# Tile-0 exponentials, the pacing of the second tail and the routing schedule of a one-core decoder block moved

## The chip, the cores and the metric

One core of a Trainium2 chip runs the whole program. The metric is the device time of one execution in microseconds (us); the time before is the median of three runs.

## The reference

One hybrid decoder layer on 512 tokens of width 2048, all in float32. Cut to what matters here:

```python
h = rms_norm(x, g[0]) * (1 + scale1) + shift1
y = hybrid_mixer(h, ...)              # attention + convolution branches, sigmoid gates, w_out
x = x + gate1 * rms_norm(y, g[1])
h = rms_norm(x, g[2]) * (1 + scale2) + shift2
q = h @ w_q                           # 8 heads, two halves of 128
s1, s2 = q halves @ sub_keys          # 128 scores each
v1, i1 = top_k(s1, 16); v2, i2 = top_k(s2, 16)
top, ci = top_k(v1[:, None] + v2[None, :], 16)
expert = i1[ci // 16] * 128 + i2[ci % 16]
gate = softmax(top)
act = gelu(h . expert_down[expert]) * gate      # 128 experts for each token
y = sum(act * expert_up[expert])
x = x + gate2 * rms_norm(y, g[3])
```

For each of the 512 tokens 128 rows of `expert_down` and 128 rows of `expert_up`, of 8 KB each, are gathered from memory: 2 x 512 gathers of 1 MB.

## The kernel before

The program has a first part (projections, attention, convolution) that the change doesn't touch, and then, on each of five engines, an order written out by hand.

**Two tails.** `tail(0)` does the rest of the mixer, the norms, the queries and the key scores for the first 128 tokens (tile 0), `tail(1)` the same for the other 384 (tiles 1 to 3). A tail reads its weights in chunks of 1 MB (0.5 MB for `ao`): four times the groups `ga` (4 chunks), `gc` (4), `ao` (2), `co` (2), then `out` (16), `x` (one for each tile), and then the queries `q`: 16 chunks. In `tail(1)` the queries come twice: `q` for tile 1 (16 chunks in four groups, each followed by the scores `sc` of two heads) and `q2` for tiles 2 and 3 (16 more). That is 99 chunks. SyncE issues them into a ring of three buffers in `tail(1)`; a buffer comes free when TensorE has used it.

**Retrieval.** It runs over 512 blocks `b`, 128 for each tile. For each block GpSimd gathers a row set from `down` (into `d_row`) and, 22 blocks later in its own order, one from `up` (into `u_row`). VectorE does `dot(b)` on `d_row`, line 1633; ScalarE the gelu of 16 dots and the weights (`block_weights`, line 1170); TensorE `weighted_rows(b - 24)` on `u_row`. GpSimd's queue is in order: a gather that waits holds all behind it. A `down` gather waits for the dot that last used its buffer and, at the first 32 blocks of a tile, for the routing of the heads that it needs (`routed`); an `up` gather waits for TensorE's use of its buffer. Both rings have three buffers up to block `WIDE` and five after it, and block `WIDE` itself waits for the end of `tail(1)`. At every 32nd block TensorE and ScalarE (line 1158) lay out the next 32 tokens of `h`, after all dots of the 32 before.

**Routing.** `route(t, n, step)`, six steps, takes two heads of tile `t` from scores to expert numbers on VectorE; step 3 releases ScalarE's `gate_exp(t, n)` (line 1151), and `gates(t, n)` on VectorE (lines 1619 to 1624) waits for that exponential. Tiles 0 and 1 are routed inside their tails; tiles 2 and 3 in `retrieve`, between dots, from the 28th block of the tile before on, with 24 blocks for each pair of heads.

**Pacing.** All engines place the retrieval inside `tail(1)` by one table: behind chunk `i` of `tail(1)` each goes on to block `PACE[i]` (`passed`, `chunk_out`). ScalarE goes by lumps of 3, 4 and 5 chunks, VectorE by lumps of 9, 2 and 1 in the gate groups and 4 in the queries. Before, `PACE` is 6, 8, 16, 19, 21 behind chunks 2, 3, 8, 10 and 11, 118 behind the last `x` chunk, 120, 123, 125 and 128 behind the four `q` groups, and 156 behind the last `q2` group.

**End of tail(0).** VectorE ends it with `route(0, 3)`, `gates(0, 2)` and `gates(0, 3)`, and then goes on to `tail(1)`, whose first act is `passed(1, 9)`: the first dots. ScalarE's `gate_exp(0, 3)` stands behind the four `ga` sigmoids (line 1222) of the first group of `tail(1)`. TensorE's `co` group of each round of four waits for VectorE's products on the `ao` group (line 1700), which stand behind the dots of `passed(c, 9)`.

Of the kernel before, what the change touches and what calls it, by code (L numbers as in the profile page):

```python
# [20 lines left out]
TT = S // P  # L21
# [15 lines left out]
def tail_groups(c):  # L37

    out = [(kind, cg, k) for cg in range(4) for kind, k in (("ga", 4), ("gc", 4), ("ao", 2), ("co", 2))]
    out += [("out", i, 4) for i in range(4)] + [("x", t, 1) for t in range(TAIL[c][1] // P)]  # L40
    for go, _, _ in QUERIES[c]:
        out += [(kind + go, i, k) for i in range(4) for kind, k in (("q", 4), ("sc", 0))]
    return out
# [3 lines left out]
BLOCKS = GROUPS * 32  # L47
LAG = 24
UP_LAG = 22
WIDE = 160  # L50
END = BLOCKS + 64


C_ID = 0
# [77 lines left out]
def block_pace():  # L132


    work = [k * (12 if kind in ("ga", "gc", "co", "out") else 6 if kind == "ao" else 9 if kind == "x" else 4) / max(k, 1)
            for kind, _, k in tail_groups(1) for _ in range(k)][:-16]
    out = [round(128 * at / sum(work)) for at in itertools.accumulate(work)]
    return out + [128 + 7 * (i + 1) // 4 for i in range(16)]


PACE = block_pace()
# [60 lines left out]
def block_kernel(nc, x, ada_w, ada_rows, w_in, w_attn_o, w_conv_o, w_out, w_q, down, up, keysT, pos, small, const, out):  # L202
# [9 lines left out]
    with ctx:  # L212
# [808 lines left out]
        def _(act):  # L1021
# [126 lines left out]
            def gate_exp(t, n):  # L1148
                act.wait_ge(gap2_ready, 4 * t + n + 1)
                g_ = gate[:, 2 * n:2 * n + 2, :]  # L1150
                A(g_, g_, ACT.Exp).then_inc(exp2_ready, 1)
# [32 lines left out]
            def retrieve(upto):  # L1184
                nonlocal pos_
                while pos_ < upto:
                    b = pos_
                    if b % 32 == 0 and b < BLOCKS:
                        h2_quarters(b // 32)
                    unit = b // 16 - 1  # L1190
                    if 0 <= 16 * unit < BLOCKS:
                        if b % 16 == 3:
                            unit_gelu(unit)
                        if 7 <= b % 16 < 15:
                            block_weights(16 * unit + 2 * (b % 16 - 7))
                            block_weights(16 * unit + 2 * (b % 16 - 7) + 1)
                    J = b // 32 - 1
                    if 0 <= J < GROUPS and b % 32 == 24:
                        z_squares(J)
                    if 0 <= J < GROUPS and b % 32 == 26:  # L1200
                        z_std(J)
                    t, n = b // 128 + 1, (b % 128 - 44) // 24
                    if 2 <= t < TT and b % 128 >= 44 and (b % 128 - 44) % 24 == 0 and n < 4:
                        gate_exp(t, n)
                    pos_ += 1

            chunk_at = 0
# [7 lines left out]
            def tail(c):  # L1215
                t0, n = TAIL[c]
                tok = slice(t0, t0 + n)
                for cg in range(4):
                    passed(c, 3)
                    for m in range(4):  # L1220
                        act.wait_ge(g_done, DONE[c, "ga", cg] + m + 1)
                        A(mixT[:, mix_at(4 * cg + m), tok], ps[:, m, 0:n], ACT.Sigmoid).then_inc(act_took, 1)
                    if c == 0 and cg == 0:
                        conv_activation()
                    if c == 1 and cg == 0:
                        gate_exp(0, 3)
                    passed(c, 4)
                    for m in range(4):
                        act.wait_ge(g_done, DONE[c, "gc", cg] + m + 1)
                        if c or cg:  # L1230
                            act.wait_ge(mix_ready, 16 * c + 4 * cg)
                        elif m == 0:
                            act.wait_ge(lnsq_done, 1)
                        A(sgc[:, m, 0:n], ps[:, m, 0:n], ACT.Sigmoid).then_inc(act_took, 1)
                    if c == 0 and cg == 0:
                        for t in range(TT):
                            attention_turned(t)
                    passed(c, 5)
                for i in range(4):
                    passed(c, 3)  # L1240
                    for m in range(4):
                        act.wait_ge(g_done, DONE[c, "out", i] + m + 1)
                        A(hT[:, 4 * i + m, tok], ps[:, m, 0:n], ACT.Copy)
                        if i == 0 and m == 0:
                            act.wait_ge(mix_ready, 16 * (c + 1))
                        if i and m == 0:
                            act.wait_ge(sqs_used, 10 * c + i)
                        A(sqt[:, m, 0:n], ps[:, m, 0:n], ACT.Square).then_inc(act_took, 1)
                    passed(c, 1)
                act.wait_ge(ss_done, 2 * c + 1)  # L1250
                A(row[:, 0:n], ps[:, 6, 0:n], ACT.Sqrt, scale=1.0 / D, bias=eps).then_inc(std2_ready, 1)
                passed(c, n // P)
                act.wait_ge(dve_took, VTOOK[c, "x", n // P - 1] + 4)
                for kk in range(8):
                    if kk >= 2:
                        act.wait_ge(sqs_used, 10 * c + 3 + kk - 1)
                    A(sqt[:, 2 * (kk % 2):2 * (kk % 2) + 2, 0:n], mixT[:, 2 * kk:2 * kk + 2, tok], ACT.Square).then_inc(sq2_ready, 1)  # L1257
                act.wait_ge(ss_done, 2 * c + 2)
                A(row[:, 0:n], ps[:, 6, 0:n], ACT.Sqrt, scale=1.0 / D, bias=eps).then_inc(std2_ready, 1)
                for k in range(KT):  # L1260
                    act.wait_ge(h2n_ready, 4 * c + k // 4 + 1)
                    A(hT[:, k, tok], hT[:, k, tok], ACT.Identity, scale=modc[:, 2, k:k + 1], bias=modc[:, 1, k:k + 1]).then_inc(h2_ready, 1)  # L1262
                for go, q0, qn in QUERIES[c]:
                    for i in range(4):
                        passed(c, 3)
                        for m in range(4):
                            act.wait_ge(g_done, DONE[c, "q" + go, i] + m + 1)
                            if m == 0 and i:
                                act.wait_ge(g_done, DONE[c, "sc" + go, i - 1] + 4)
                            elif m == 0 and go:  # L1270
                                act.wait_ge(g_done, DONE[c, "sc", 3] + 4)
                            A(sqt[:, m, 0:qn], ps[:, m, 0:qn], ACT.Copy).then_inc(act_took, 1)
                        for m in range(4):
                            act.wait_ge(g_done, DONE[c, "sc" + go, i] + m + 1)
                            for t in range(q0 // P, (q0 + qn) // P):
                                ins = A(sc[t][:, 4 * i + m, :], ps[:, m, t * P - q0:(t + 1) * P - q0], ACT.Copy)
                            ins.then_inc(act_took, 1)
                        passed(c, 1)
                        if not go and i:
                            gate_exp(c, i - 1)  # L1280
                    if c and not go:
                        gate_exp(c, 3)
                if c == 0:
                    act.wait_ge(g3_done, 1)
                    A(g3r, ps[:, 7, :], ACT.Copy).then_inc(g3_ready, 1)
# [7 lines left out]
        def _(dve):  # L1293
# [27 lines left out]
            for q in range(4):  # L1321
                for i in range(4):
                    n = 8 * q + 2 * i
# [335 lines left out]
            def retrieve(upto):  # L1659
                nonlocal pos_  # L1660
                while pos_ < upto:
                    b = pos_
                    J = b // 32 - 1
                    if 0 <= J < GROUPS and b % 32 == 28:
                        finish(J)
                    if b < BLOCKS:
                        dot(b)
                    unit = b // 16 - 1
                    if b % 16 == 5 and 0 <= 16 * unit < BLOCKS:
                        unit_act(unit)  # L1670
                    t, n = b // 128 + 1, (b % 128 - 28) // 24
                    if 2 <= t < TT and b % 128 >= 28 and n < 4:
                        step = (b % 128 - 28) % 24
                        if step % 2 == 0 and step < 12:
                            route(t, n, step // 2)
                        if step == 20:
                            gates(t, n)
                    pos_ += 1
# [9 lines left out]
            def tail(c):  # L1688
# [56 lines left out]
                for i in range(4):  # L1745
# [3 lines left out]
                        route(c, i, step)  # L1749
                    if i:  # L1750
                        gates(c, i - 1)
                gates(c, 3)
                if c:
                    for _ in range(4):
                        passed(c, 4)

# [67 lines left out]
```

## Time and profile before

| what | us |
|---|---|
| median of 3 runs (lowest, highest) | 4117.74 (4116.97, 4125.35) |
| the profiled execution, its own time | 4122.73 |
| its span | 4120.9 |
| PE busy | 2794.8 |
| DVE busy | 2276.4 |
| POOL busy | 1410.1 |
| ACT busy | 544.5 |
| moved by DMA | 1430.07 MB, mean 347 GB/s |

PE is TensorE's matmul, PEld its weight load, DVE is VectorE, ACT ScalarE, POOL GpSimd and SP SyncE. Times in the rows are us from the span's start unless they are marked ns. A number in square brackets behind a row is how long the engine was idle before it, with what ended that. "DMA share" is the mean busy share of the 16 DMA engines; a stretch in which they are all busy shows 1.01.

### The profile page before, as it was taken

To read this page: it belongs to the slowest core of one execution; us is meant where nothing else is said; L and a number is where in the kernel's file an instruction comes from. 1 tells how busy PE (TensorE), PEld (TensorE's weight loads), DVE (VectorE), ACT (ScalarE), POOL (GpSimd) and SP (SyncE) were. 2 spreads that over 40 slices of the span, in tenths; PEclk is the share of its full clock that TensorE was granted. 3 is DMA by queue.
4 is the path that set the end of the run, shared out by engine and by line. 5 is a ranking of instruction groups with operands and counts; after the bars stand their busy time and mean duration, and the time that the engine had idled before them with its cause. 6 is when DMAs were issued, how large, how long until landed. Compare 5 with 4: busy or idle time off the path is not lost.

```text
span 4120.9 us, 38729 instructions
## 1 busy us (share of the span) xinstructions
PE 2794.8 (68%) x15652; PEld 1651.8 (40%) x15652; DVE 2276.4 (55%) x3525; ACT 544.5 (13%) x1207; POOL 1410.1 (34%) x1109
## 2 busy tenths in 40 slices
PE   5999899899898999998878443443444434444435
PEld 3787788789754555554755110110100101101101
DVE  6399779742554333335754566654665564444442
ACT  3211221200210111111211111010101100100000
POOL 2421211000013344333134554435434435444342
PEclk9999999999999999999989555555555555555556
DMA  9353323798558999989889999999999999999998
GB/s 367 145 225 122 154 104 141 269 408 331 208 207 338 386 403 378 410 343 385 339 332 420 385 404 421 422 421 421 421 421 417 421 421 415 420 422 420 421 422 369
DMA packets 204145, 1430.07 MB, mean 347 GB/s; under 512 B 24640, under 2 KB 24768, under 8 KB 32192
## 3 DMA queue, kind: packets, MB, share of 16 engines
q0 software_dynamic: 152064, 1107.36, 65.2%
q1 hardware_dynamic: 45984, 308.30, 19.3%
q10 hardware_dynamic: 5920, 11.94, 0.8%
q8 instruction: 124, 2.03, 0.2%
q14 instruction: 53, 0.43, 0.0%
HBM read 1420.13 MB, written 7.39 MB: 346 GB/s over the span
## 4 chain that ended last, share of the span: by engine, by line
PE 40%; DMA 38%; DVE 13%; POOL 4%; issue 3%; ACT 2%; ACTq 0%; another core or an unknown queue 0%; DVEq 0%; SPq 0%; POOLq 0%
PE psum L621 40%; DMA front<-in_down,back 28%; DMA front<-in_up,back 8%; DVE front L1633 4%; POOL front L592 3%; DVE back L1400 2%; DMA front<-in_w_conv_o 1%; DVE back L1369 1%; ACT back L1158 1%; POOL x_low L576 1%; DMA back<-in_x 1%; DVE back L1734 0%; ACT front L1262 0%; DVE back L1569 0%; DVE back L1563 0%
## 5 line engine op out<-in xcount | busy, mean ns | idle before, releaser
L621 PE MATMUL psum<-front 128*32 128x512 f32 (+3 forms) x7120 | 1383.3, 615 | 855.5 <-DMA front<-in_up,back 789.2
L1633 DVE CUSTOM_DVE_ANT_0 front<-front,back 128x2048 f32<-128x2048 f32 x512 | 1170.8, 2292 | 1318.0 <-DMA front<-in_down,back 1150.0
L621 PEld LDWEIGHTS psum<-front 128*128 128x128 f32 (+1 forms) x7120 | 626.4, 162 | 1546.4 <-issue 1327.2
L592 POOL DMA_INDIRECT front<-in_down,back x512 | 603.7, 1179 | 909.7 <-DVE back L1633 665.0
L621 PE MATMUL psum<-back,front 128*32 128x128 f32 (+3 forms) x4400 | 641.3, 459 | 351.2 <-DMA back<-in_up,back 172.7
L592 POOL DMA_INDIRECT front<-in_up,back x442 | 526.3, 1191 | 941.3 <-PE psum L621 891.4
L621 PEld LDWEIGHTS psum<-back,front 128*32 128x32 f32 (+1 forms) x4400 | 374.3, 168 | 627.4 <-issue 348.4
L570 POOL TENSOR_TENSOR w_low<-front,w_high 128x2048 fp32r<-128x2048 f32 x33 | 155.2, 4704 | 539.4 <-ACT w_high L1046 539.4
L621 PE MATMUL psum<-x_high,w_high 128*128 128x512 f32 x640 | 252.6, 395 | 9.2 <-POOL x_low L576 6.4
L621 PE MATMUL psum<-x_high,w_low 128*128 128x512 f32 x640 | 251.0, 392 | 0.0
L621 PE MATMUL psum<-x_low,w_high 128*128 128x512 f32 x640 | 250.9, 392 | 0.0
L621 PE MATMUL psum<-back 128*32 128x128 f32 (+5 forms) x1400 | 180.5, 388 | 48.4 <-ACT back L1257 11.7
L1170 ACT ACTIVATE front<-back 128x32 f32<-128x32 f32 x512 | 116.0, 308 | 717.7 <-DVE back L1642 717.7
L621 PEld LDWEIGHTS psum<-back 128*128 128x128 f32 (+1 forms) x1400 | 134.0, 182 | 125.6 <-issue 58.4
L1369 DVE SCALAR_TENSOR_TENSOR back<-back 128x512 f32<-128x512 f32 x232 | 160.1, 759 | 0.0
L1046 ACT ACTIVATE w_high<-front 128x2048 fp32r<-128x2048 f32 x52 | 99.6, 1916 | 456.9 <-PE psum L621 407.8
L1400 DVE SCALAR_TENSOR_TENSOR back<-back 128x512 f32<-128x512 f32 x120 | 145.1, 1209 | 7.6 <-DMA back<-in_ada_w 2.2
L621 PEld LDWEIGHTS psum<-x_high,w_high 128*128 128x128 f32 x640 | 121.6, 190 | 36.3 <-POOL x_low L576 7.5
L621 PEld LDWEIGHTS psum<-x_low,w_high 128*128 128x128 f32 x640 | 121.5, 190 | 25.2
L621 PEld LDWEIGHTS psum<-x_high,w_low 128*128 128x128 f32 x640 | 121.3, 189 | 25.5
L1158 ACT ACTIVATE back<-psum 128x512 f32<-128x512 f32 x64 | 38.2, 597 | 613.1 <-DVE back L1633 383.1
L592 POOL DMA_INDIRECT back<-in_up,back x70 | 82.2, 1174 | 90.3 <-PE psum L621 85.1
(161 smaller groups left out, 1676.3 us busy)
## 6 DMA issues: line engine op xcount, KB each, us to landing
front<-in_w_in SPq DMA_DIRECT2D x116, 1024.0 KB, 5.0
back<-in_ada_w SPq DMA_DIRECT2D x64, 1024.0 KB, 7.9
front<-in_w_q SPq DMA_DIRECT2D x48, 1024.0 KB, 4.8
front<-in_ada_rows POOLq DMA_DIRECT2D x32, 1024.0 KB, 13.7
front<-in_w_out SPq DMA_DIRECT2D x32, 1024.0 KB, 4.9
front<-in_w_conv_o SPq DMA_DIRECT2D x16, 1024.0 KB, 16.1
front<-in_w_attn_o SPq DMA_DIRECT2D x16, 512.0 KB, 11.6
front<-in_down,back POOLq DMA_INDIRECT x512
```

Of the source, the lines that this page charges most:

```text
L570: nc.gpsimd.tensor_tensor(wl[s], ring[s], wh[s % 2].bitcast(fp32), ALU.subtract).then_inc(w_low_done, 1)
L576: nc.gpsimd.tensor_tensor(x_low[:, k, :], h_tmp[k % 2], x_high[:, k, :].bitcast(fp32), ALU.subtract).then_inc(hT_ready, 1)
L592: nc.gpsimd.indirect_dma_start(out=row_, out_offset=None, in_=table[:, :], in_offset=bass.IndirectOffsetOnAxis(ap=idx4[:, t % 2, c:c + 1], ...
L621: return nc.tensor.matmul(o, a, b, start=start, stop=stop)
L1046: A(wh[s % 2], ring[s], ACT.Copy).then_inc(w_high_done, 1)
L1158: A(h2r[:, i * NT:(i + 1) * NT], ps[:, 7, :], ACT.Copy).then_inc(h2r_ready, 1)
L1170: A(diag[:, b % 32, :], same[:, 0:32], ACT.Copy, scale=actv[:, n % 2, b % 16:b % 16 + 1]).then_inc(diag_ready, 1)
L1369: last[c] = st.did(V.scalar_tensor_tensor(total, src, tap, total, ALU.mult, ALU.add))
L1400: ins = V.scalar_tensor_tensor(total, part, weight, total, ALU.mult, ALU.add)
L1633: V.tensor_tensor_reduce(d_row[s], d_row[s], h2r, 1.0, 0.0, ALU.mult, ALU.add, pre[:, b // 16 % 2, b % 16:b % 16 + 1]).then_inc(dots_done, 1)
```

## The change

The exponential of the last two heads of tile 0 goes ahead of the first `ga` sigmoids of `tail(1)` on ScalarE, and its `gates(0, 3)` goes from the end of `tail(0)` to behind dot 3 on VectorE. `PACE` reaches block 128 behind the first `q` group (chunk 70) and no longer behind the fourth; it stays there for the second, reaches 132 behind the third and 138 behind the fourth (ten dots of tile 1), and 162 at the end of `q2`. Behind the last `x` chunk it is 125. Behind chunks 2, 3, 8, 10 and 11 it is 6, 8, 17, 20 and 22. `WIDE` goes from 160 to 168. The routing of tiles 2 and 3 begins at the 36th block instead of the 28th, with 23 blocks for each pair of heads instead of 24.

```diff
-WIDE = 160
+WIDE = 168
 END = BLOCKS + 64
+ROUTE, STRIDE = 36, 23
@@ block_pace
-            for kind, _, k in tail_groups(1) for _ in range(k)][:-16]
+            for kind, _, k in tail_groups(1) for _ in range(k)][:-28]
     out = [round(128 * at / sum(work)) for at in itertools.accumulate(work)]
-    return out + [128 + 7 * (i + 1) // 4 for i in range(16)]
+    out += 4 * [128] + [129, 130, 131, 132, 133, 135, 136, 138]
+    return out + [138 + 3 * (i + 1) // 2 for i in range(16)]
@@ ScalarE, retrieve
-                    t, n = b // 128 + 1, (b % 128 - 44) // 24
-                    if 2 <= t < TT and b % 128 >= 44 and (b % 128 - 44) % 24 == 0 and n < 4:
-                        gate_exp(t, n)
+                    t, at = b // 128 + 1, b % 128 - ROUTE - 16
+                    if 2 <= t < TT and at >= 0 and at % STRIDE == 0 and at < 4 * STRIDE:
+                        gate_exp(t, at // STRIDE)
@@ ScalarE, tail
                     passed(c, 3)
+                    if c == 1 and cg == 0:
+                        gate_exp(0, 3)
                     for m in range(4):
                         act.wait_ge(g_done, DONE[c, "ga", cg] + m + 1)
                         A(mixT[:, mix_at(4 * cg + m), tok], ps[:, m, 0:n], ACT.Sigmoid).then_inc(act_took, 1)
                     if c == 0 and cg == 0:
                         conv_activation()
-                    if c == 1 and cg == 0:
-                        gate_exp(0, 3)
@@ VectorE, retrieve
-                    t, n = b // 128 + 1, (b % 128 - 28) // 24
-                    if 2 <= t < TT and b % 128 >= 28 and n < 4:
-                        step = (b % 128 - 28) % 24
+                    if b == 3:
+                        gates(0, 3)
+                    t, at = b // 128 + 1, b % 128 - ROUTE
+                    if 2 <= t < TT and 0 <= at < 4 * STRIDE:
+                        n, step = at // STRIDE, at % STRIDE
@@ VectorE, tail
-                gates(c, 3)
                 if c:
+                    gates(c, 3)
                     for _ in range(4):
                         passed(c, 4)
```

## Rows read from the trace of the kernel before

**Rows 1.** The page: DMA busy tenths and rate in 40 slices.

```profile
DMA  9353323798558999989889999999999999999998
GB/s 367 145 225 122 154 104 141 269 408 331 208 207 338 386 403 378 410 343 385 339 332 420 385 404 421 422 421 421 421 421 417 421 421 415 420 422 420 421 422 369
```

**Rows 2.** Windows: busy us and count of each engine, clock, DMA share, GB/s.

```profile
1130.00:1250.00 120.00, 100.85 (x419) 59.70 (x420) 73.41 (x195) 12.60 (x20) 23.12 (x16) 0.93 0.59 224
1250.00:1950.00 700.00, 671.75 (x2933) 355.54 (x2932) 279.43 (x314) 78.78 (x196) 263.01 (x198) 0.98 0.95 383
1950.00:1980.00 30.00, 15.23 (x87) 12.05 (x86) 13.74 (x9) 13.90 (x23) 1.87 (x2) 0.72 0.14 50
1980.00:2060.00 80.00, 74.77 (x653) 63.93 (x651) 67.35 (x257) 13.57 (x53) 16.83 (x15) 1.00 1.01 419
2060.00:2093.00 33.00, 10.88 (x126) 8.32 (x127) 31.42 (x130) 4.00 (x7) 6.96 (x5) 0.64 0.43 163
2270.00:2310.00 40.00, 15.85 (x164) 6.34 (x156) 23.88 (x56) 3.89 (x6) 18.43 (x15) 0.63 0.82 327
2310.00:4110.00 1800.00, 756.55 (x4606) 168.10 (x4606) 960.47 (x1433) 164.93 (x505) 807.68 (x712) 0.54 1.01 419
```

**Rows 3.** Timeline around the last exponential of tile 0.

```profile
1152.87 0.19 DVE L1596 TENSOR_TENSOR back<-back 128x32 f32<-128x32 f32 x1
1160.55 2.73 DVE L1624 TENSOR_TENSOR back<-back 32x8 f32<-32x8 f32 x16
1173.58 0.49 ACT L1222 ACTIVATE back<-psum 128x384 f32<-128x384 f32 x1 [21.49 <-PE psum L621]
1183.39 0.19 DVE L1619 TENSOR_REDUCE back<-back 128x2 f32<-128x32 f32 x1 [20.10 <-ACT back L1151]
1186.58 2.29 DVE L1633 CUSTOM_DVE_ANT_0 front<-front,back 128x2048 f32<-128x2048 f32 x1
```

**Rows 4.** Timeline around the first `ao` and `co` groups.

```profile
1222.40 10.48 PE L621 MATMUL psum<-back,front 128*128 128x384 f32 x32
1222.60 5.49 SPq L507 DMA_DIRECT2D front<-in_w_conv_o  x2
1247.44 1.94 DVE L1700 TENSOR_TENSOR back<-back,psum 128x384 f32<-128x384 f32 x4
1248.13 12.21 PE L621 MATMUL psum<-back,front 128*128 128x384 f32 x28 [15.24 <-DVE back L1700]
```

**Rows 5.** DMA issues of the page: count, size, us to landing.

```profile
front<-in_w_in SPq DMA_DIRECT2D x116, 1024.0 KB, 5.0
front<-in_w_conv_o SPq DMA_DIRECT2D x16, 1024.0 KB, 16.1
```

**Rows 6.** Groups by form, 1160 to 1222, TensorE; and one `weighted_rows`, timeline.

```profile
L621 PE MATMUL psum<-front 128*128 128x384 f32 x194 | 62.7, 486 | 0.0
1378.52 1.07 PE L621 MATMUL psum<-front 128*32 128x512 f32 x8
```

**Rows 7.** Waits from 1250 to 1940: total us, times, longest.

```profile
DVE front L1633 <- ACT back L1158: 37.5, 3, 15.0
```

**Rows 8.** Timeline of the queries and the routing of tile 1.

```profile
1976.80 0.94 POOL L592 DMA_INDIRECT front<-in_up,back  x1 [31.53 <-PE psum L621]
...
1989.84 0.87 DVE L1555 MAX8 back<-back 128x8 f32<-128x128 f32 x4 [20.89 <-ACT back L1276]
...
2065.54 2.24 POOL L592 DMA_INDIRECT front<-in_down,back  x1 [21.58 <-DVE back L1633]
...
2080.68 1.93 PE L621 MATMUL psum<-back,front 128*32 128x128 f32 x32 [21.51 <-ACT back L1158]
...
2093.34 2.29 DVE L1633 CUSTOM_DVE_ANT_0 front<-front,back 128x2048 f32<-128x2048 f32 x1
...
2153.25 2.29 DVE L1633 CUSTOM_DVE_ANT_0 front<-front,back 128x2048 f32<-128x2048 f32 x1 [3.60 <-DMA front<-in_down,back]
```

**Rows 9.** The chain of waits, start and us: the first dot behind `route(1, 0)`.

```profile
2007.69 2.29 DVE front L1633
```

## The prediction

> **What bounds the kernel.** I read the page's 40 slices first: from slice 12 on the DMA engines are busy nine tenths or more of nearly every slice, and from slice 21 on they move 420 GB/s [rows 1]. The stages show why: from 2310 to 4110 us the DMA share is 1.01 with every compute engine far from full, PE 757 of 1800 us and DVE 960 [rows 2]. This is the stream of 1024 gathers. None of them is added or removed, so in this part of the program the end moves by one thing: the time in which the DMA engines stand idle before it. I therefore count idle DMA time, length x (1 - share/1.01), in each window [rows 2]: 1130 to 1250: 49.9 us. 1250 to 1950: 41.6. 1950 to 1980: 25.8. 1980 to 2060: 0. 2060 to 2093: 19.0. 2270 to 2310: 7.5. 2310 to 4110: 0. Some 144 us in all. A stall of an engine counts only if it is in one of these holes.
>
> **Part 1, the exponential of tile 0.** Step 3 of `route(0, 3)` has its gate differences at 1153.06, but ScalarE stands in front of the `ga` sigmoids, whose sums come at 1173.58; VectorE waits 20.10 us for the exponential, does `gates(0, 3)` (1183.39 to 1186.54, 3.15 us), and only then starts dot 0 at 1186.58 [rows 3]. Afterwards the exponential runs at about 1154, some 20 us ahead of the first sigmoid, so its 0.23 us and its table load have cover and TensorE isn't touched; the cover would have to shrink by 18 us before this cost anything. VectorE ends `gates(0, 2)` at 1163.28 [rows 3] and goes straight to dots 0 to 2, whose data landed long before. All dots and gathers of the first round start 1186.58 - 1163.28 = 23.3 us earlier. The moved `gates(0, 3)` lies behind dot 3, where VectorE waits for gathers.
>
> How much survives? The next meeting is line 1700. Dots 0 to 15 ran until 1247.44, then the `ao` products; TensorE had ended `ao` at 1232.88 and stood 15.24 us, to 1248.13 [rows 4]. Now there is a 17th dot (`PACE[8]` is 17, was 16), about 4 us with its gather, so VectorE is there at 1247.44 - 23.3 + 4 = 1228, ahead of TensorE. The first product takes some 0.6 us, so TensorE can go on at 1233.5: 14.6 us earlier. Above that nothing is won, since from here on TensorE's chunks set the pace. It could be less: the `co` chunk is issued at 1222.60 [rows 4], and such chunks took 16.1 us to land, against 5.0 for `w_in` [rows 5]. At 16.1 it lands at 1238.7 and the gain is 9.4; at 5.0 it lands in time and the gain is 14.6. I take the middle, **12 us**, because fewer gathers are in flight here than in later rounds (the `up` gathers start only at block 22).
>
> The Trainium skill (DMA: Bandwidth & Descriptors, "Queues, rings and completion order") has each DMA engine go round-robin between the queues that have work, packet by packet. By that rule the chunk would get half the rate and land in time, and part 1 would be worth 14.6; the 16.1 us of the row speak for the 9.4.
>
> **Part 2, eight more blocks ahead of the routing.** A gate chunk costs TensorE 32 matmuls, 62.7/194 x 32 = 10.3 us, and each `weighted_rows` 1.07 us [rows 6]. At 1.89 blocks for each chunk (before) that is 12.3 us; the DMA engines need 1 + 2 x 1.89 = 4.79 MB-chunks of 1.049 MB at 421 GB/s [rows 1], 2.49 us each: 11.9 us. The two are level. Now 2.01 blocks go with each chunk: 12.5 us for TensorE and 12.5 for DMA. So the stage gets longer (by T0, the start of `route(1, 0)`, about five more blocks have been gathered, 25 us of transfers), but these are transfers that fall away later. What counts is its 41.6 us of holes. Three of them are the 32-block boundaries, where VectorE waits for the new rows of `h`, 37.5 us in all [rows 7]; they stay, as does the start without `up` gathers. I take **3 us** for the rest; bounds are -3 (the boundaries fall at other chunks) and +8.
>
> **Part 3, the queries and the routing.** The hole from 1950 to 1980 is the norm chain, with GpSimd held 31.53 us behind TensorE [rows 8]; it stays. The other one is the end of the routing. Before, with T0 = 1989.84 [rows 8], the first routing took 17.8 us, to 2007.69 [rows 9]; four of them, four gates of 3.15 and 8 dots of 2.29 make 102, measured 2093.34 - 1989.84 = 103.5. In its last 33 us all stood at once: GpSimd 21.58 us behind a dot, and TensorE 21.51 us behind the layout at line 1158, which ScalarE did only after `gate_exp(1, 2)`, that is, after most of `route(1, 3)` [rows 8]. That made 19.0 us of idle DMA.
>
> Now block 128 is crossed in the third query group. The order that I work out: GpSimd reaches `down` gather 128 at the last `x` chunk and is held until `route(1, 0)` has ended, T0 + 17.8. From 19 us before T0 to there DMA has 8 weight chunks and 3 gathers, 11 x 2.49 = 27 of 37 us: 10 idle, where before it was 6.5 (1970 to T0): **3.5 us lost**. Then the layout for block 128 at T0 + 20 to 30; dots 128 to 131 behind `route(1, 1)`, with some 5 us of waiting for gather 131; `route(1, 2)` to T0 + 71; dots 132 to 137 until T0 + 92, the last three each waiting for a gather; `route(1, 3)` and gates to T0 + 116. In these 98 us DMA has 13 `down`, 13 `up` and 12 weight transfers, 38 x 2.49 = 95 us. One stall sits in it: ScalarE comes to block weight 112 before it takes the fourth group's queries, and that waits for `unit_act` at dot 133, T0 + 79; TensorE stands some 15 us, but 3 weight buffers and 6 gather buffers are then still filling. I allow 5 us idle. So the 19.0 us become 5: 14.0 won, 3.5 lost, **10.5 us**. Bounds: 15.5 (nothing idle behind T0 + 17.8), -5 (the old 19.0 and 5 besides).
>
> **Part 4, the rest.** `WIDE` 168 keeps three buffers for eight more blocks while the weights still run; the hole at 2270 to 2310, where block 160 is laid out, is 7.5 us [rows 2] and stays or grows. Routing of tiles 2 and 3 starts 8 blocks later and ends at block 125 of 128, ahead of the first gather that needs it by more than the ring; it is 21 us of VectorE in 23 blocks of 5 us. **0 us**; bounds -5 (the hole nearly doubled) and +3.
>
> **Sum.** 12 + 3 + 10.5 + 0 = 25.5 us. The profiled execution took 4122.7, so its like would take 4097.2; the median of three is 5 us under it, so 4117.7 - 25.5 = **4092 us**. A check from the other side: before, dot 138 began at 2153.25 [rows 8]. Now it begins near T0' + 116 with T0' = 1990 - 12 + 25 - 3 = 2000, so 2116, 37 us earlier, with about 4 or 5 weight chunks fewer moved (11 us): 26.
>
> **Rivals.**
> - *The routing stretch fills fully and so do the boundaries*: parts at their upper bounds, 14.6 + 8 + 15.5 + 3 = 41, or 4077. For it: the hole before 2093 has one clear cause, ScalarE's order [rows 8]. Against it: part 2 has only the 41.6 us, mostly bound to boundaries. 0.2.
> - *Only the start gains*: the new stall of TensorE at `unit_act`, T0 + 64 to T0 + 79, lets the rings run full, and the hole of 19 us moves there. Then 9.4 to 14.6 remains: 4105. For it: GpSimd's queue is in order and the rings have three buffers. Against: 38 transfers are there for 39 places. 0.15.
> - *No change*: the start's gain is eaten as well, by `co` weights at 16.1 us or more and a longer hole at block 160, with the routing hole unchanged; between 4110 and 4126. 0.08.
> - *Slower*, one mechanism: GpSimd held at gather 128. It is decided by the time from the last `x` chunk to the end of `route(1, 0)`: were TensorE there to stand for `up` rows stuck behind gather 128, the 37 us would hold only 8 chunks, 17 us idle instead of 6.5; the hole of 19.0 would stay, and a second like it open where TensorE stands for `unit_act`. 12 - 10.5 - 19 = -17.5: 4135. The point is T0' + 30: if the layout of block 128 ends later than that, it begins to hold. TensorE's work at T0 needs no row beyond 103, so I give it 0.04.
> - The forecast has the other 0.53.
>
> **Numbers.** A measurement of this kernel can tell a change of about 0.2%, 8 us, from none. The forecast's own range is 4083 to 4102. Taking in the two neighbours and leaving the rest out gives 4075 to 4108. Faster: 0.53 + 0.2 + 0.15, less a little at the edge: 0.87. Same 0.08, slower 0.05.
>
> **What would show it.** Right: dot 0 near 1163, no wait of VectorE for line 1151; the first `co` matmul at 1233 to 1239; an idle DMA time of some 38 us instead of 49.9 in the first stage; tile-1 dots between the routings; the share of the 33 us before the last gates above 0.9; GpSimd's longest wait at gather 128. Wrong: a new idle stretch of DMA above 10 us in the query groups, or a hole at block 160 above 12 us; or a stage 1250 to 1950 whose holes grow by more than 5 us.

## The result and the profile after

The changed kernel takes 4072.2 us in the median of its four runs (4068.97 to 4079.01), beside 4119.59 before: ratio 0.9882, 95% interval 0.9864 to 0.9899. Run again on another chip it took 4078.98 beside 4124.02, ratio 0.9896 (0.9880 to 0.9912). So it is 43 to 49 us faster. The forecast was 4092, 25.5 us, with a range of its own of 4083 to 4102, and 4075 to 4108 with its two neighbours. The direction was right, the sum was short by about 20 us, and below it is shown that two of its terms were too small and one too large.

The stream of gathers behind the tail has not changed (421 GB/s, as in [rows 1]). What changed lies before it. To compare I cut both executions at the same events: the first `ga` matmul of `tail(1)`; the first `ga` matmul of its second round; the norm chain (its first reciprocal); the first operation of `route(1, 0)`, called T0; then T0 + 130, + 330 and + 560. The windows of the kernel before, with busy us and count of each engine, granted clock, DMA share and GB/s:

```profile
1131.80:1271.80 140.00, 122.61 (x481) 72.08 (x482) 79.53 (x196) 12.60 (x20) 25.93 (x19) 0.93 0.61 230
1271.80:1913.80 642.00, 629.48 (x2789) 332.68 (x2787) 240.89 (x244) 73.51 (x189) 248.54 (x187) 0.99 0.95 384
1913.80:1989.80 76.00, 45.49 (x253) 31.21 (x252) 44.43 (x73) 21.17 (x39) 15.41 (x13) 0.78 0.66 270
1989.80:2119.80 130.00, 100.85 (x837) 81.22 (x837) 110.40 (x397) 18.90 (x65) 35.94 (x29) 0.91 0.86 350
2119.80:2319.80 200.00, 143.69 (x856) 92.82 (x854) 92.85 (x131) 26.36 (x92) 81.37 (x68) 0.84 0.98 402
2319.80:2549.80 230.00, 91.73 (x522) 17.86 (x522) 140.92 (x277) 19.41 (x54) 123.15 (x94) 0.52 1.00 414
```

And of the changed kernel:

```profile
1128.30:1250.20 121.90, 119.75 (x481) 70.80 (x482) 81.95 (x199) 10.05 (x18) 29.88 (x21) 0.99 0.74 281
1250.20:1902.60 652.40, 636.98 (x2855) 334.09 (x2853) 254.96 (x255) 76.20 (x204) 263.76 (x200) 1.00 0.98 399
1902.60:1979.80 77.20, 43.47 (x284) 30.87 (x285) 48.07 (x76) 19.87 (x38) 12.09 (x11) 0.78 0.64 264
1979.80:2109.80 130.00, 103.74 (x798) 81.17 (x796) 109.18 (x397) 21.14 (x65) 39.67 (x29) 0.89 0.91 360
2109.80:2309.80 200.00, 142.92 (x858) 90.07 (x858) 91.69 (x130) 23.29 (x79) 87.94 (x69) 0.82 0.97 401
2309.80:2539.80 230.00, 97.16 (x564) 21.16 (x564) 147.26 (x285) 23.58 (x69) 121.42 (x97) 0.51 1.01 421
```

Read the last column: length x (1 - GB/s / 421) is the time for which the DMA engines' full rate was not used. This is a little more than the idle time by the share, since it also counts slow stretches.

| stage | before | after | won |
|---|---|---|---|
| first round | 63.5 | 40.5 | 23.0 |
| rounds 2 to 4, `out`, `x` | 56.4 | 34.1 | 22.3 |
| norm chain, first queries | 27.3 | 28.8 | -1.5 |
| routing, T0 to + 130 | 21.9 | 18.8 | 3.1 |
| to + 330 (block 160) | 9.0 | 9.5 | -0.5 |
| to + 560 | 3.8 | 0 | 3.8 |
| sum | 181.9 | 131.7 | 50.2 |

The spans differ by 52.2 us (4120.9 and 4068.7). Both profiles are of one execution, and not of the median one: 4122.73 before, 5 us above the median of the first three runs, and 4070.52 after, 1.7 us below the median. In the second run's profile (`e9_after_again`), cut in the same way, the six figures are 40.1, 37.4, 30.7, 20.7, 10.5 and 0: 42.5 us won, with 44.1 between the spans (4120.9 and 4076.8). So the measure follows the span in both, and a few us in a stage are the difference between two executions.

The first round in the timeline of the changed kernel:

```profile
1149.41 0.19 DVE L1599 TENSOR_TENSOR back<-back 128x32 f32<-128x32 f32 x1
1149.64 0.23 ACT L1154 ACTIVATE back<-back 128x32 f32<-128x32 f32 x1 [2.04 <-DVE back L1599]
1159.86 2.29 DVE L1636 CUSTOM_DVE_ANT_0 front<-front,back 128x2048 f32<-128x2048 f32 x1
...
1170.39 0.49 ACT L1227 ACTIVATE back<-psum 128x384 f32<-128x384 f32 x1 [19.22 <-PE psum L624]
...
1219.21 31.12 PE L624 MATMUL psum<-back,front 128*128 128x384 f32 x96
...
1250.17 12.09 PE L624 MATMUL psum<-front 128*128 128x384 f32 x37
```

The exponential runs as soon as its input is there, 20.7 us ahead of the first sigmoid, and dot 0 starts at 1159.86 (in this execution the stage begins 3.5 us earlier than before; over all profiles it begins between 1125.9 and 1132.5, whatever the change, so this is not a gain). TensorE now goes through `ao` and `co` without a stop, where [rows 4] had 15.24 us.

### The profile page after: what moved, and what is told of

The parts are those of the page before. It is cut to its first block, busy times and chain, and to the rows that moved or that the text cites. A ratio compares the mean times of both kernels' runs of the same rounds, so it can differ in the third digit from the quotient of the medians.

```text
span 4068.7 us, 38721 instructions
## 1 busy us (share of the span) xinstructions
PE 2782.0 (68%) x15652; PEld 1644.1 (40%) x15652; DVE 2275.8 (56%) x3525; ACT 539.8 (13%) x1203; POOL 1408.8 (35%) x1109
## 3 DMA queue, kind: packets, MB, share of 16 engines
q1 hardware_dynamic: 45984, 308.30, 19.5%
## 4 chain that ended last, share of the span: by engine, by line
PE 41%; DMA 39%; DVE 12%; POOL 3%; issue 3%; ACT 2%; ACTq 0%; DVEq 0%; SPq 0%; POOLq 0%
PE psum L624 40%; DMA front<-in_down,back 27%; DMA front<-in_up,back 10%; DVE front L1636 3%; POOL front L595 3%; DVE back L1403 2%; DVE back L1372 1%; DMA front<-in_w_in 1%; DMA back<-in_ada_w 1%; ACT back L1161 1%; DMA back<-in_up,back 1%; DMA back<-in_x 1%; DMA front<-in_w_conv_o 0%; DVE back L1739 0%; ACT front L1265 0%
## 5 line engine op out<-in xcount | busy, mean ns | idle before, releaser
L624 PEld LDWEIGHTS psum<-front 128*32 128x32 f32 (+1 forms) x7136 | 627.0, 162 | 1558.3 <-issue 1336.3
L624 PE MATMUL psum<-back,front 128*32 128x128 f32 (+3 forms) x4384 | 625.5, 445 | 296.9 <-DMA back<-in_up,back 169.0
L624 PEld LDWEIGHTS psum<-back,front 128*32 128x32 f32 (+1 forms) x4384 | 365.0, 163 | 565.9 <-issue 317.2
```

What stands on the lines that cost most here:

```text
L624: return nc.tensor.matmul(o, a, b, start=start, stop=stop)
```

## The experiments

All variants were timed against the kernel before on the same chip. The ratio counts; medians on different chips differ by some us.

**The parts one at a time.** `e1_exp_alone` is the kernel before with the four hunks of the exponential:

```diff
+                    if c == 1 and cg == 0:
+                        gate_exp(0, 3)
                     for m in range(4):
                         act.wait_ge(g_done, DONE[c, "ga", cg] + m + 1)
...
-                    if c == 1 and cg == 0:
-                        gate_exp(0, 3)
...
+                    if b == 3:
+                        gates(0, 3)
...
-                gates(c, 3)
                 if c:
+                    gates(c, 3)
```

> The kernel before with only the exponential of tile 0 ahead of the first sigmoids and its gates behind dot 3; PACE, WIDE and the routing schedule as before. Theory 1 (the first term of the sum was undersized: TensorE's 15.24 us stall goes whole, and with it 3 to 6 us of slower matmuls behind it): 17 to 22 us faster than before, about 4100. Theory 2 (the first term holds, 9.4 to 14.6 us, and the surplus of the change over the forecast comes from the pacing): 4105 to 4110.

Measured: 0.9954 (0.9937 to 0.9971), 4106.57 beside 4125.45, 18.9 us. The median speaks for theory 1; the interval reaches to 12 us and does not exclude theory 2 by itself. The trace adds the place: 123.2 us from the first `ga` matmul to that of the second round, where before took 140.0. That is 16.8 us, already more than the 14.6 which the forecast held for the most.

`e2_no_exp` undoes these hunks in the changed kernel:

> The changed kernel with the exponential and gates(0, 3) back in their old places: the pacing, WIDE and the routing schedule alone. Theory 1: 17 to 22 us slower than the changed kernel, 4090 to 4094, so the pacing is worth some 27 to 30 us. Theory 2: 9 to 15 us slower, 4081 to 4087, the pacing is worth 33 to 38. If the two parts help each other, the sum of both gains alone is clearly less than 47.

Measured: 0.9944 (0.9927 to 0.9960), 25.3 us. 18.9 and 25.3 make 44.2, against 43 to 49 for both: within the noise the parts add up. By the ratios the exponential is worth 20 to 26 us in the changed kernel. The 25.3 us are what pacing, `WIDE` and routing schedule give together, where the forecast had 13.5 (3, 10.5 and 0).

`e3_no_ten` keeps the dense first stage and takes the dots of tile 1 out of the routing:

```diff
-    out += 4 * [128] + [129, 130, 131, 132, 133, 135, 136, 138]
-    return out + [138 + 3 * (i + 1) // 2 for i in range(16)]
+    out += 12 * [128]
+    return out + [128 + 17 * (i + 1) // 8 for i in range(16)]
```

> The changed kernel, but PACE stays at 128 through the second, third and fourth query group and then rises evenly to 162 over the 16 chunks of q2: tile 0 ends as early, but no dot of tile 1 lies in the routing. The forecast's third term: the ten dots fill the idle DMA at the end of the routing, so without them 10 to 15 us slower than the changed kernel, 4082 to 4087, with a DMA hole of 20 us or more ahead of the last gates. Rival (the surplus is the dense first stage, and the ten dots are worth little): 4072 to 4077.

Measured: 0.9928 (0.9911 to 0.9944), 30.4 us, so 13 to 19 us behind the changed kernel. Its routing stretch (T0 to + 130):

```profile
1987.50:2117.50 130.00, 103.82 (x799) 87.21 (x799) 99.89 (x388) 18.26 (x61) 25.09 (x22) 0.92 0.76 297
```

38.3 us unused, against 18.8. On top of the dense first stage the ten dots do what the forecast's third term said, and are worth more than its 10.5. (The edit also lets `PACE` rise faster in `q2`, 34 blocks over the 16 chunks instead of 24; the 19.5 us lie ahead of that, in the routing stretch.)

`e6_exp_dense` is the first experiment and the dense first stage alone; `e14_half_dense` goes half the way:

```diff
e6:  -            ... for _ in range(k)][:-16]
     +            ... for _ in range(k)][:-28]
     +    out += 12 * [128]
          return out + [128 + 7 * (i + 1) // 4 for i in range(16)]
e14: the same with [:-22] and 6 * [128]
```

> The kernel of the first experiment (exponential alone) with the dense first stage besides: PACE at 128 by the first query group, there through the other three, then 7/4 blocks a chunk to 156 as before; WIDE 160, routing schedule as before. Forecast: the second term, 3 us won, with the routing hole of 19 us unchanged or longer: 4103 within 5 us against 4106 without. Theory 1: the dense stage alone gives nothing or loses up to 10 us, since the transfers of the eight blocks leave the routing stretch. Theory 2 (the surplus lies here): 10 us or more won.

> The exponential alone plus half of the dense stage: PACE reaches 128 behind chunk 76, the middle of the third query group, instead of chunk 82 (before) or 70. Theory 1 (in the first stage TensorE's pace left the DMA engines short of work, and each block more fills a part of it): idle DMA from the second round to the norm chain between the 65 us of the exponential alone and the 39 us of the dense one, near 52, and the idle time in the routing between 24 and 42. Theory 2 (the 26 us come from where the 32-block boundaries happen to fall): near 65 or near 39, not between.

Measured: `e6_exp_dense` 0.9937 (0.9921 to 0.9954), 24 to 26 us faster than before, about 7 more than the exponential alone (the intervals overlap); `e14_half_dense` 0.9962 (0.9950 to 0.9975), 15.5 us. The 7 us lie between the forecast's 3 and the 10 of theory 2, and the half step seems slower than no step; so the totals settle nothing. The windows of the two stages say more. For each kernel rounds 2 to 4 with `out` and `x`, then T0 to + 130. The exponential alone:

```profile
1252.10:1904.70 652.60, 633.64 (x2797) 334.57 (x2795) 241.10 (x244) 74.12 (x190) 257.39 (x188) 0.99 0.94 379
1980.20:2110.20 130.00, 100.35 (x824) 80.73 (x822) 110.49 (x397) 18.90 (x65) 33.81 (x27) 0.89 0.85 342
```

Half dense:

```profile
1253.30:1905.70 652.40, 634.50 (x2821) 334.50 (x2819) 245.85 (x248) 72.77 (x189) 260.28 (x192) 0.99 0.96 386
1982.30:2112.30 130.00, 105.42 (x839) 88.07 (x832) 103.90 (x394) 17.36 (x59) 27.20 (x24) 0.91 0.79 316
```

Dense:

```profile
1253.30:1910.60 657.30, 638.73 (x2855) 335.03 (x2853) 254.77 (x257) 76.18 (x204) 258.92 (x200) 0.99 0.97 396
1988.90:2118.90 130.00, 107.52 (x808) 90.30 (x806) 98.18 (x387) 17.35 (x57) 22.49 (x19) 0.91 0.73 286
```

| | first stage unused | routing unused |
|---|---|---|
| exponential alone | 65.1 | 24.4 |
| half dense | 54.2 | 32.4 |
| dense | 39.0 | 41.7 |
| dense and ten dots (the changed kernel) | 34.1 | 18.8 |

The first column falls step by step, as theory 1 of the half-dense run said (near 52 was expected, 54.2 measured). The first three rows can be compared with each other: each profile is of the slowest run of its kernel, 7 to 8 us above its median. The fourth, and the kernel before with its 56.4 and 21.9, are of other places in their runs, so that the 65.1 may be some us high beside them. The second column rises by 17 as the first falls by 26: the blocks gathered earlier are missing in the routing stretch, and the ten dots take that back. The dense stage alone is worth about 7 us; together with the ten dots, `WIDE` and the routing schedule 24 to 30. The ten dots without the dense stage were not run.

Does the number of gathers for each chunk fill the stage, or the place where the 32-block boundaries fall? The waits of VectorE at the three boundaries between 1250 and 1940 (total us, times, longest) fall too. Before has 37.5 [rows 7]; half dense:

```profile
DVE front L1634 <- ACT back L1159: 33.3, 3, 13.5
```

and the changed kernel:

```profile
DVE front L1636 <- DMA front<-in_down,back: 375.5, 91, 9.9
DVE front L1636 <- ACT back L1161: 17.2, 3, 6.6
```

Such a wait is also a hole of the DMA engines. The windows of 20 us to either side of the second boundary's first dot, before and after:

```profile
1558.33:1598.33 40.00, 37.85 (x258) 20.83 (x257) 11.48 (x10) 6.15 (x9) 14.01 (x10) 1.00 0.80 318
```

```profile
1514.51:1554.51 40.00, 37.85 (x263) 20.55 (x262) 17.53 (x20) 3.89 (x6) 16.14 (x12) 1.00 0.89 361
```

Before, GpSimd's queue stands there too, for a buffer that TensorE has to free, and in the 10 us from 1570 the engines move 134 GB/s:

```profile
1578.79 2.64 POOL L592 DMA_INDIRECT front<-in_up,back  x1 [14.64 <-PE psum L621]
```

Three such windows of 40 us, one for each boundary, hold a good part of what the stage leaves unused:

| | VectorE's three waits | unused at the boundaries | unused in the rest of the stage |
|---|---|---|---|
| before | 37.5 | 30.2 | 26.2 |
| exponential alone | 40.5 | 30.8 | 34.3 |
| half dense | 33.3 | 27.3 | 26.9 |
| dense | 19.8 | 19.7 | 19.3 |
| changed | 17.2 | 18.7 | 15.4 |
| changed, second profile | 21.2 | 21.9 | 15.5 |

Away from the boundaries the unused time falls in even steps with the number of gathers, 34.3, 26.9, 19.3, which theory 1 says and theory 2 doesn't. At the boundaries it falls with VectorE's waits, mostly in the second step, and there the place of the boundary in the chunks is not excluded: each of the three can fall well or badly by itself. So the stage has two causes of about equal size, of which the first shows in three profiles and the second is not taken apart.

**`WIDE`.** Beside a control, these runs change only this number, or the order in which the five buffers are taken.

> The changed kernel with WIDE back at 160. The forecast's fourth term: 0, within 3 us of the changed kernel. Rival: block 160 comes ahead of the end of the tail now, GpSimd's queue stands there until the last query group is done, and it costs 5 us or more.

> The kernel before with WIDE 168 alone. Theory 1 (the fourth term is only worth something together with the pacing: with 160 and a PACE that ends at 162, gather 160 holds GpSimd's queue until the last chunk): within 4 us of before, since there PACE ends at 156. Theory 2 (gather 160 holds the queue in the kernel before as well, and WIDE 168 is worth the same 14 us in either): 4108 to 4112.

> The changed kernel with WIDE 176. If WIDE pays only by lying behind the end of the tail, it is within 3 us of the changed kernel. If the three buffers kept for eight blocks longer cost, 3 to 8 us slower. If 168 was still too near, faster by 3 or more.

> The changed kernel itself once more, as a control: its four first runs were on another chip than the variants of it. If they stand for it, the ratio to before is 0.988 again, some 48 us. If they were lucky by 8 us or so, it is 0.990 to 0.992, and what the variants with WIDE 160 and 176 and the old routing schedule seemed to lose shrinks by as much.

> The changed kernel with WIDE 160 once more, on the same chip as the control. If WIDE 168 is worth what the first comparison seemed to show, 12 to 16 us slower than the control; if half of that was between chips, 4 to 9 us; if the fourth term of the forecast holds, within 3.

Measured: `e4_wide160` 0.9918 (0.9901 to 0.9934) and again `e10_wide160_again` 0.9919 (0.9905 to 0.9932), while the changed kernel on the same chip (`e9_after_again`) had 0.9896. Side by side 160 costs 4089.46 - 4078.98 = 10.5 us, between the two sizes that the run's expectation named, and 160 is not within 3 us. The control itself has 0.9896 instead of 0.9882, so all that was read against the first run of the changed kernel shrinks by up to 6 us. `e5_wide_only`: 0.9985 (0.9975 to 0.9995), 6 us for 168 in the kernel before, between its two theories. `e7_wide176`: 0.9915 (0.9898 to 0.9932), some 8 to 13 us worse than 168 by the ratios, though its interval overlaps the control's.

With 160, two windows are worse than in the changed kernel. From T0 + 130 to + 330 both profiles with 160 have 14.7 us unused, against 9.5 and 10.5; from + 330 to + 560 they have 3.8 and 4.4, against 0 and 0. GpSimd's queue has a long wait in each. The first line is from the second run with 160, the second from the first:

```profile
2244.77 0.94 POOL L595 DMA_INDIRECT front<-in_down,back  x1 [16.54 <-PE psum L624]
```

```profile
2365.62 0.94 POOL L595 DMA_INDIRECT front<-in_up,back  x1 [11.66 <-PE psum L624]
```

The first is the `down` gather of block 160 behind the end of `tail(1)`. The second comes 22 blocks later, at the `up` gather of block 160, when the `up` ring changes. In the table of buffers the first block on five buffers takes buffer 0. With 160 the block that had buffer 0 last is 159, one back, so the gather waits for work that has just been queued; with 176 it is two back, with 168 three.

> The changed kernel with WIDE 171. In the table of buffers the first block on five buffers takes buffer 0; the block that had it last is 159 for WIDE 160 (one back), 174 for 176 (two back), and three back for 168 and 171, the multiples of three. Theory 1 (this is what WIDE is worth): within 4 us of the changed kernel, and no DMA hole when the up ring changes, 22 blocks later. Theory 2 (168 is simply the right distance behind the tail): 4 us or more slower.

> The changed kernel with WIDE 160, the five buffers taken up in the order 1, 2, 0, 3, 4, so that blocks 160 to 162 follow blocks 157 to 159. Theory 1: the hole near 2360 us (4 to 5 us in both runs with WIDE 160) goes, and the time comes within 6 us of the changed kernel; what is left is gather 160 behind the end of the tail. Theory 2: no better than with WIDE 160 in the plain order, 10 us or more behind the changed kernel.

> The changed kernel with WIDE 168 and the buffers taken up in the order 3, 4, 0, 1, 2: the two new ones first. If the hole of 8 to 10 us at block 160 is only a matter of buffers, nothing changes, since block 168 comes later; within 3 us of the changed kernel. If the rings run short right behind the tail, 3 to 6 us faster.

`e12_wide160_oldest` and `e13_fresh_first` change the table (here for the first, on `WIDE = 160`; the second has `(3, 4, 0, 1, 2)` on 168):

```diff
-def slot_table(count, change, few, more):
+def slot_table(count, change, few, more, order=None):
...
         s = b % few if b < change else (b - change) % more
+        if order and b >= change:
+            s = order[s]
...
-D_SLOT = slot_table(BLOCKS, WIDE, 3, len(D_KB))
-U_SLOT = slot_table(BLOCKS, WIDE, 3, len(U_KB))
+D_SLOT = slot_table(BLOCKS, WIDE, 3, len(D_KB), (1, 2, 0, 3, 4))
+U_SLOT = slot_table(BLOCKS, WIDE, 3, len(U_KB), (1, 2, 0, 3, 4))
```

Measured: 171 0.9911 (0.9895 to 0.9928), 160 with the oldest buffer first 0.9905 (0.9888 to 0.9921), the fresh ones first 0.9902 (0.9886 to 0.9919). The window from T0 + 330 to + 560 shows the hole of the `up` ring. With 160 in the plain order, then with the oldest first:

```profile
2319.20:2549.20 230.00, 93.24 (x529) 19.51 (x533) 144.34 (x282) 23.57 (x69) 116.64 (x95) 0.53 0.99 413
```

```profile
2318.80:2548.80 230.00, 96.65 (x564) 21.21 (x564) 147.04 (x284) 23.57 (x69) 117.60 (x97) 0.51 1.01 421
```

4.4 us against 0, and 0 in the changed kernel; the order of the buffers is the cause of that hole. It also was a hole of the kernel before (3.8 us), and is most of the 6 us of `e5_wide_only`. The window ahead of it falls from 14.7 to 10.5 as well, though the `down` gather of block 160 waits 16.54 us in `e12_wide160_oldest` too: that wait behind the end of the tail is not what costs. How the order acts in that window is not shown. The two windows make 8.6 of the 10.5 us.

171, three back as well, has 6.0 us unused from + 330 to + 560, against theory 1 of its run, and 176 has 7.6. The trace says where: not when their rings change, but at the boundary at block 192. Both lose nearly all of it from 2404 to 2414, in 171:

```profile
2404.60:2414.60 10.00, 5.92 (x96) 2.93 (x88) 4.65 (x4) 3.29 (x5) 3.75 (x2) 0.84 0.47 170
```

```profile
2410.55 2.73 POOL L595 DMA_INDIRECT front<-in_up,back  x1 [12.31 <-PE psum L624]
```

The gathers counted from the first, this is the `up` gather of block 171, in 176 as well (13.84 us). It is still on three buffers in effect and needs the one of block 168, whose rows TensorE takes only behind the layout of block 192. With 168 the gathers of blocks 171 and 172 go into the two new buffers ahead of this layout; the next one waits only 7.67 us, and no 10 us fall below 416 GB/s there:

```profile
2406.82 2.16 POOL L595 DMA_INDIRECT front<-in_up,back  x1 [7.67 <-PE psum L624]
```

So 168 avoids two holes, one from the order at 160 and one from changing too late for block 192. The second is read from traces and no run tests it by itself. It also leaves open how much of the totals it makes: by the ratios 171 is 6 to 12 us behind the changed kernel, but the intervals overlap. `e12_wide160_oldest` and `e13_fresh_first` are within the control's interval, so no version beats the changed kernel.

**The routing schedule.** `e8_route28` has `ROUTE, STRIDE = 28, 24` in the changed kernel.

> The changed kernel with the routing schedule of before (28th block, 24 blocks a pair). Routing of tile 2 would then start at block 156, ahead of the scores, which come at the end of the tail at 162: VectorE stands at block 156 until the last scores are copied, and gathers stop: 10 to 25 us slower than the changed kernel. Rival: VectorE is there only as the tail ends anyway: within 5 us.

Measured: 0.9929 (0.9909 to 0.9950), 13 to 19 us behind. VectorE's waits from 2200 to 2270:

```profile
DVE back L1558 <- ACT back L1279: 20.0, 1, 20.0
```

It stands at block 156 for the last scores, and the window from T0 + 130 to + 330 has 23.3 us unused, against 9.5. 36 blocks instead of 28 are what the new end of `PACE`, 162, makes necessary; what they are worth in the kernel before was not run.

## Why the prediction was wrong

The way of counting held: the unused DMA time fell by 50.2 us and the span by 52.2. (The 40 slices were read a little too kindly: slices 12, 17, 19 and 20 show 8 tenths, and 22 and 23 show 385 and 404 GB/s. No term rests on that.) The terms did not hold. By the windows, part 1 won 17 us for 12, part 2 some 28 for 3, part 3 about 2 for 10.5, part 4 some 3 for 0. The error of part 2 alone is as large as that of the sum; those of the other parts cancel in the main.

**Part 1, the exponential: right mechanism, size too small.** 12 us were forecast, 18.9 measured alone, with 14.6 as the most. Two things were missed. The `co` weights were in time: TensorE runs from `ao` into `co` without a gap, 96 matmuls in 31.12 us in both profiles of the changed kernel and with the exponential alone, so the middle between 9.4 and 14.6 was a wrong choice. The 16.1 us of [rows 5] could not price this chunk: the second profile of the changed kernel has the same median of 16.1, and no gap. And TensorE's stop had a price behind it. In the kernel before the granted clock was 0.63 from 1233 to 1248 and 0.87 from 1248 to 1272, and the `co` group took 23.82 us; in the changed kernel the clock from 1229 to 1251 was 1.00, its higher level, and the same 64 matmuls take 20.6 (31.12 less the 10.5 of `ao`): 3.2 us more. In two other profiles with the stop (`e2_no_exp` and `e5_wide_only`) they take 22.30 and 23.10, so 1.7 and 2.5 us more. 15.24 and 3.2 are the 18.4 us by which this round got shorter (18.1 measured). The Trainium skill (DMA: Bandwidth & Descriptors, "Queues, rings and completion order") has a DMA engine take its queues in turn, packet by packet. The prediction's working from it gave the better end of the range, 14.6; the runs show that no wait for the chunk arose, not how the queues share.

**Part 2, the dense stage: the step that failed.** The prediction took 41.6 us of idle DMA in this stage, and set against them "Three of them are the 32-block boundaries, where VectorE waits for the new rows of `h`, 37.5 us in all [rows 7]; they stay". That left 4 us to win from, and it took 3. Two things were wrong. The holes at the boundaries did not stay: they fell from 30.2 to 18.7 us (21.9 in the second profile), and VectorE's waits from 37.5 to 17.2. And an engine's wait was set for the hole. By the share, the measure that the 41.6 is in, the three windows of 40 us have 24.2 idle and not 37.5, so that 17.4 were left elsewhere. There the unused time, by the rate, fell by another 10.8 us, and it falls with the number of gathers. By the windows this stage won 22.3 us. The first round won another 6 by its 17th dot and the gathers with it (the exponential alone has 46.5 unused there, the dense kernels 40), of which the forecast had nothing.

Why the waits at the boundaries got shorter no run shows. At the second one VectorE now has six us of `ao` products to do (1524.12 to 1529.95) while TensorE comes to the layout; before it had nothing there.

The check from the other side also gave the stage the full 25 us of the added transfers: T0 was forecast at 2000 and came at 1979.8 (1986.0 in the second profile). From before, the first round is 18.1 us shorter and the next stage only 10.4 longer.

**Part 3, the routing: right course, too much won.** The order worked out for after T0 is nearly what the trace shows. Tile-1 dots begin at 2018.74, T0 + 38.9, where two routings of 17.8 us and a gate of 3.15 put them; dot 131 waits 5.38 us for its gather (5 forecast); dot 132 is at 2054.10, T0 + 74.3 (T0 + 71 and a gate); GpSimd's longest wait behind T0 is that at gather 128:

```profile
POOL front L595 <- DVE back L1614: 26.6, 1, 26.6
PE psum L624 <- DMA front<-in_up,back: 14.6, 4, 5.5
PE psum L624 <- ACT back L1275: 5.1, 1, 5.1
```

The stall of TensorE for `unit_act` is 5.1 us, not 15. But the unused time in this stretch fell only from 21.9 to 18.8 (19.3 to 12.9 by the share), and in the stage ahead of it, where gather 128 begins to wait, it rose by 1.5. The holes are now other ones: 5.5 us from 1980 to 2000, where gather 128 is held, 5.3 from 2050 to 2070, around TensorE's stall of 5.1, and 7.1 from 2090 to 2110, whose cause is open. Against a dense stage without them the ten dots are worth 19 us in this stretch: the forecast priced parts 2 and 3 apart, but they are one trade.

**Part 4: 0 forecast, 2 to 3 measured in all,** but not because nothing lies there. The hole at block 160 stayed (9.0 and 9.5), and the later one of 3.8 went. With the new pacing, `WIDE` left at 160 costs 10.5 us, and the routing left at 28 costs 13 to 19.

**The check from the other side** agreed with the sum because it used the sum's own terms for T0. Dot 138 came at 2101.2, not at 2116, 52.1 us earlier than in [rows 8]; that is the difference of the spans, and of the 11 us which the check took off for weight chunks still to move nothing is left at the end. Why is open.

**The rivals.** The one at the upper bounds gave 4077 and had 0.2; even it was too small: its 14.6 left out the slow matmuls behind the stop, and its +8 for part 2 was far under the 28. Gather 128 does hold the queue, as the slower rival said, but the layout of block 128 ended at T0 + 25.7, ahead of T0 + 30, and the price stayed in the 18.8 us.

## What to carry to other kernels

If a stream of transfers sets the end, count for each stage the part of the full rate that is not used, and take it from the DMA columns of the stage. An engine's wait tells where a hole may be, not how large it is, and not that it stays when the schedule around it moves. Moving transfers into such a stage pays in full only if something else fills the place that they leave: compare the pair of stages, not each alone. When a ring changes its depth, look at which buffer the first block takes, since one that was used just before makes the deeper ring start with a stall, and at which stall comes next, since the ring should be deep before it.

## What the runs showed of the hardware

A stop of TensorE of 15.24 us cost 3.2 us more behind its end, in matmuls at a mean granted clock of 0.87 in place of 1.00; after stops of 14.70 and 18.34 us it was 2.5 and 1.7 us.

The medians from issue to landing of a 1 MB weight chunk don't follow the kernel. In seven of the sixteen profiles `w_in` has 4.9 to 5.2 us and `w_conv_o` 14.6 to 17.0, in the other nine 7.2 to 8.5 and 8.0 to 9.4. The kernel before is in the first group, and the changed kernel in both: 8.4 and 9.4 in one profile, 5.1 and 16.1 in the other, with TensorE's first round of about the same length (121.9 and 121.6 us). What divides the groups is not shown; a median of this kind over other places is a poor price for one transfer.
